# A two-layer hybrid block in fp32 on one core: the Hyena stage cut into nine short steps a block, with the filters' last layer as fp32r in two halves

## The chip, the cores and the metric

The kernel runs on one core of a Trainium2 chip. The metric is the device time of one execution in microseconds. Each engine of the core (TensorE or PE, VectorE or DVE, ScalarE or ACT, GpSimd or POOL, and SyncE or SP, which here only issues DMAs) runs its own program in order; they meet through semaphores.

## The reference

Two layers over 256 tokens of width 2048. Nearly all the work is dense products with weights. Beside them stand, in the first layer, a Hyena branch and an mLSTM branch, in the second layer two further mixers. The change touches the Hyena branch alone:

```
...
    h = jnp.sin(f1.astype(f32) * (z @ w1.astype(f32) + b1.astype(f32)))
    h = jnp.sin(f2.astype(f32) * (h @ w2.astype(f32) + b2.astype(f32)))
    h = h @ w3.astype(f32)
...
    return h.reshape(L, HYENA_ORDER, 2, HYENA_WIDTH) * window[:, None, None, :]
...
def long_conv(u, kf, bias):
    L = u.shape[1]
    uf = jnp.fft.rfft(u, n=2 * L, axis=1)
    y = jnp.fft.irfft(uf * kf[None], n=2 * L, axis=1)[:, :L]
    return y + u * bias
...
        z = hx1 * long_conv(hv, kf[:, 0], hb[0])
        y_a = (hx2 * long_conv(z, kf[:, 1], hb[1])).astype(x.dtype)
```

w3 is 64 x 4096. The filters are two orders by four quarters of 256 channels: eight blocks.

## The kernel before

Every weight matrix streams through SBUF in DMAs of 1 MB (RAW). One such piece is two units, and a unit is eight tiles of 128x128 (`tiles` walks over them, `w.i` counts them). For each unit u, ACT rounds the raw weights to fp32r (WH, L1144), and the rest, raw minus WH, goes to WL: on DVE for even u (L1747), on POOL for odd u (L2557). The activations are split in the same way (HNH and HNL), and `group` multiplies in fp32r WH by HNH (L599), WH by HNL (L600) and WL by HNH (L603). WH and WL have four slots. ACT's program rounds unit v+3 where its own walk comes to tile 8v, but first waits until PE has finished unit v-1. DVE and POOL make the WL of unit v+3 at tile 8v+1, after the WH. So the three stay close to PE's place, and SP issues the next raw piece when both WL of the piece before in that buffer are done.

Beside this stream, a class `Walk` runs a generator ("side") on each engine: `beside(side, rate, skip)` sets how many of its steps fall on 16 tiles and how many are left out first. Every engine has its own `hyena()` with the same count of steps, so step n stands at the same tile in all five programs (on PE after the four tiles it is in). The projections of the first layer (56 pieces, 896 tiles, fourteen groups of 64 tiles) carry the Hyena stage.

Before the change the rate is 1.04 steps on 16 tiles (1.12 from tile 385 on): a step on 15.4 or 14.3 tiles. Three steps make the small network (PE L684 and L690, DVE's range reduction, ACT's sine) and the filters of block 0. A block then has six steps (five for the last):

- step 0: PE transposes the inputs (L707) and transforms the filters (KT, L713); ACT copies both (L1193, L1199); POOL adds and subtracts the halves (KS, L2597 and L2598)
- step 1: PE transforms the inputs (L720), ACT copies one half (L1204), DVE makes UP (L1853)
- step 2: DVE multiplies M (L1859) and adds Y (L1862)
- step 3: DVE multiplies and subtracts the second half (L1866, L1869), POOL adds and subtracts Y into UP (L2604, L2605)
- step 4: PE multiplies the next block's filters, `filters`, 64x128 by 64x512 in fp32 (L677); DVE windows them (L1815); POOL makes HSD (L2583, L2584); SP loads WIN and W3
- step 5: PE's inverse transform (L735), DVE gates the result (L1884, L1890 or L1893), and for the last four blocks ACT and DVE split it into YAH and YAL

In several steps, then, one engine waits for another within the step. In group g, two further things stand at fixed tiles: at tile 16 PE transposes the outputs of the group before (`turn_projected`, L617), and at tiles 18 to 22 ACT and DVE do a short convolution on them (L1433, L1797, L1802).

PSUM: three banks for the stream, five (PB3 to PB7) in turn for everything beside it; PE waits before it takes a side bank until what was in it five turns earlier has been read.

## Time and profile before

| | us |
|---|---|
| median of 3 runs | 2712.99 (2712.69 to 2713.46) |
| the profiled execution | 2712.05, its span 2710.1 |
| PE busy | 2669.4, 98% of the span |
| ACT busy, POOL busy, DVE busy | 1245.3, 1173.8, 1028.0 |
| granted TensorE clock, mean | 0.999 |
| DMA | 488 MB, the queue of the loads busy 50.8% |

PE is busy nearly throughout, in all 40 slices of the page but the first; ACT, POOL and DVE less than half of the time, the DMA engines about half. A busy PE is still not a PE at its peak: two matmuls of the stream that follow each other overlap in the records (0.39 us each, started every 0.227 us), so time is better counted from one start to the next.

### The profile page before, as it was taken

To read this page: it belongs to the slowest core of one execution; us is meant where nothing else is said; L and a number is where in the kernel's file an instruction comes from. 1 tells how busy PE (TensorE), PEld (TensorE's weight loads), DVE (VectorE), ACT (ScalarE), POOL (GpSimd) and SP (SyncE) were. 2 spreads that over 40 slices of the span, in tenths; PEclk is the share of its full clock that TensorE was granted. 3 is DMA by queue.
4 is the path that set the end of the run, shared out by engine and by line. 5 is a ranking of instruction groups with operands and counts; after the bars stand their busy time and mean duration, and the time that the engine had idled before them with its cause. 6 is when DMAs were issued, how large, how long until landed. Compare 5 with 4: busy or idle time off the path is not lost.

```text
span 2710.1 us, 30629 instructions
## 1 busy us (share of the span) xinstructions
PE 2669.4 (98%) x12282; PEld 2197.0 (81%) x12282; DVE 1028.0 (38%) x1262; ACT 1245.3 (46%) x1584; POOL 1173.8 (43%) x535
## 2 busy tenths in 40 slices
PE   8999999999999999999999999999999999999999
PEld 6778777778888888888888878888788888888887
DVE  5556544443432223222233357335432222232222
ACT  5445444444444444444344465555454444444333
POOL 2555553344444444444444446333344444444443
PEclk9999999999999999999999999999999999999999
DMA  6444444355555555555555544454355555555554
GB/s 243 159 150 175 147 153 164 139 206 189 194 185 187 190 187 192 191 192 186 192 192 206 201 156 146 150 202 140 126 186 188 196 190 188 186 188 194 201 199 151
DMA packets 73436, 488.01 MB, mean 180 GB/s; under 512 B 8475, under 2 KB 10428, under 8 KB 15952
## 3 DMA queue, kind: packets, MB, share of 16 engines
q1 hardware_dynamic: 73296, 486.06, 50.8%
q8 instruction: 98, 1.61, 0.2%
q14 instruction: 42, 0.34, 0.0%
HBM read 483.93 MB, written 2.10 MB: 179 GB/s over the span
## 4 chain that ended last, share of the span: by engine, by line
PE 92%; DVE 2%; ACT 2%; issue 2%; POOL 1%; DMA 1%; SPq 0%; ACTq 0%; DVEq 0%; POOLq 0%
PE PB L599 28%; PE PB L603 28%; PE PB L600 28%; PE PB L617 2%; ACT WH L1144 1%; POOL WL L2557 1%; DVE WL L1747 1%; PE PB L713 1%; PE PB L720 1%; PE PB L848 0%; PE PB L735 0%; PE PB L965 0%; DMA RAW<-in_w_in_a 0%; PE PB L808 0%; DVE VY L2422 0%
## 5 line engine op out<-in xcount | busy, mean ns | idle before, releaser
L2557 POOL TENSOR_TENSOR WL<-RAW,WH 128x1024 fp32r<-128x1024 f32 x441 | 1070.2, 2427 | 1451.5 <-ACT WH L1144 1451.5
L1144 ACT ACTIVATE WH<-RAW 128x1024 fp32r<-128x1024 f32 x889 | 940.0, 1059 | 1270.6 <-PE PB L603 1256.4
L1747 DVE TENSOR_TENSOR WL<-RAW,WH 128x1024 fp32r<-128x1024 f32 x448 | 588.8, 1315 | 1522.1 <-ACT WH L1144 1521.8
L599 PE MATMUL PB<-WH,HNH 128*128 128x512 f32 x2464 | 974.2, 395 | 12.4 <-DVE MIX L2359 4.6
L603 PE MATMUL PB<-WL,HNH 128*128 128x512 f32 x2464 | 961.3, 390 | 9.1 <-POOL WL L2557 4.9
L600 PE MATMUL PB<-WH,HNL 128*128 128x512 f32 x2464 | 959.6, 389 | 0.0
L599 PEld LDWEIGHTS PB<-WH,HNH 128*128 128x128 f32 x2464 | 462.8, 188 | 120.3 <-issue 15.4
L603 PEld LDWEIGHTS PB<-WL,HNH 128*128 128x128 f32 x2464 | 462.7, 188 | 109.3 <-POOL WL L2557 6.6
L600 PEld LDWEIGHTS PB<-WH,HNL 128*128 128x128 f32 x2464 | 463.0, 188 | 92.9
L599 PE MATMUL PB<-WH,HDH 128*128 128x512 f32 x704 | 274.3, 390 | 0.0
L603 PE MATMUL PB<-WL,HDH 128*128 128x512 f32 x704 | 273.9, 389 | 0.0
L600 PE MATMUL PB<-WH,HDL 128*128 128x512 f32 x704 | 273.9, 389 | 0.0
L599 PEld LDWEIGHTS PB<-WH,HDH 128*128 128x128 f32 x704 | 132.1, 188 | 27.4
L603 PEld LDWEIGHTS PB<-WL,HDH 128*128 128x128 f32 x704 | 132.1, 188 | 27.4
L600 PEld LDWEIGHTS PB<-WH,HDL 128*128 128x128 f32 x704 | 132.2, 188 | 27.2
L599 PE MATMUL PB<-WH,MXH 128*128 128x512 f32 x128 | 50.1, 392 | 0.0
L603 PE MATMUL PB<-WL,MXH 128*128 128x512 f32 x128 | 49.8, 389 | 0.0
L600 PE MATMUL PB<-WH,MXL 128*128 128x512 f32 x128 | 49.8, 389 | 0.0
L617 PE MATMUL PB<-IDENT,TM 128*128 128x128 f32 x320 | 41.5, 273 | 0.1
L617 PEld LDWEIGHTS PB<-IDENT,TM 128*128 128x128 f32 x320 | 37.1, 140 | 5.5 <-DVE TM L2494 0.4
L2321 DVE TENSOR_TENSOR HDL<-PB,HDH 128x512 fp32r<-128x512 f32 x44 | 28.3, 686 | 13.8 <-ACT HDH L1555 13.8
L2397 DVE SCALAR_TENSOR_TENSOR TM<-PB,RTOK,TM 128x512 f32<-128x512 f32 x44 | 30.9, 743 | 0.0
(357 smaller groups left out, 1790.6 us busy)
## 6 DMA issues: line engine op xcount, KB each, us to landing
RAW<-in_w_gu SPq DMA_DIRECT2D x176, 1024.0 KB, 4.7
RAW<-in_w_dn SPq DMA_DIRECT2D x88, 1024.0 KB, 4.7
RAW<-in_w_in_a SPq DMA_DIRECT2D x55, 1024.0 KB, 4.8
RAW<-in_w_in SPq DMA_DIRECT2D x45, 1024.0 KB, 4.7
RAW<-in_w_out SPq DMA_DIRECT2D x32, 1024.0 KB, 4.7
RAW<-in_w_ga SPq DMA_DIRECT2D x24, 1024.0 KB, 4.7
RAW<-in_w_gb SPq DMA_DIRECT2D x24, 1024.0 KB, 4.7
WIN<-in_win SPq DMA_DIRECT2D x8, 512.0 KB, 5.9
```

The costliest lines, as they stand in the source:

```text
L599: e.matmul(o, hi[:, k, x], WH[:, s, c], start=k == 0, stop=False)
L600: e.matmul(o, lo[:, k, x], WH[:, s, c], start=False, stop=False)
L603: t = e.matmul(o, hi[:, k, x], WL[:, s, c], start=False, stop=k == K - 1)
L617: t = e.transpose(b[:, 256 * i + 128 * h:256 * i + 128 * h + 128], src[:, h, k:k + 128], IDENT[:, :])
L713: e.matmul(bank[:, ri * 256:(ri + 1) * 256], DF[:, c, ri, :], HSD[:, ri, c, :], start=True, stop=True).then_inc(*hy.pe.mark(("kt", blk, c, ...
L720: e.matmul(banks[c][:, ri * 256:(ri + 1) * 256], DF[:, c, ri, :], UT[:, c, :, :].rearrange("p a n -> p (a n)"), start=True, stop=True).the ...
L1144: e.activation(WH[:, u % NSPL, :], RAW[:, n % NRAW, half * SU * 128:(half + 1) * SU * 128], ACT.Copy).then_inc(*wt.act.mark(("wh", u)))
L1747: e.tensor_tensor(WL[:, u % NSPL, :], RAW[:, n % NRAW, half * SU * 128:(half + 1) * SU * 128], f32(WH[:, u % NSPL, :]), ALU.subtract).then ...
L2321: e.tensor_tensor(flat(dst[0][:, k:k + 2, :]), bank(*name, g, q)[:, :], f32(flat(dst[1][:, k:k + 2, :])), ALU.subtract).then_inc(*m.dve.ma ...
L2397: e.scalar_tensor_tensor(out=SIG[:, h, :], in0=mb(nt)[:, 0:512], scalar=RTOK[:, h:h + 1], in1=SIG[:, h, :], op0=ALU.mult, op1=ALU.mult).th ...
L2557: e.tensor_tensor(WL[:, u % NSPL, :], RAW[:, n % NRAW, half * SU * 128:(half + 1) * SU * 128], f32(WH[:, u % NSPL, :]), ALU.subtract).then ...
```

## The change

The diff does four things.

1. The Hyena stage has nine steps a block at a rate of 1.66 on 16 tiles, a step on 9.64 tiles, from tile 74 on. Nearly every result that another engine needs is used a step after it is made. The blocks' order is that of before, and the whole stage takes 86.7 tiles a block.
2. The last layer of the filters is done in fp32r. H2 and HS have 128 rows: the second half of HS holds what the first half lost in rounding. W3 is loaded twice, on 128 rows; ACT rounds it (W3H), DVE takes the rest (W3L). Two fp32r matmuls of 128x128 by 128x512 take the place of one in fp32 of 64x128 by 64x512.
3. The constants are loaded in order of use: the small network's, IDENT, the first filters, then the transforms' matrices.
4. YAH and YAL and the gating move to steps of the next block.

```diff
-        W3 = ar("W3", [64, 2, T], 36)
+        W3 = ar("W3", [128, 2, T], 36)
+        W3H = ar("W3H", [128, 2, T], 50, F32R)
+        W3L = ar("W3L", [128, 2, T], 75, F32R)
+        HS = ar("HS", [128, T], 86, F32R)
...
-            w.beside(hyena(), 1.04, 7)
+            w.beside(hyena(), 1.66, 4)
...
# tensor: filters
-                        e.wait_ge(*hy.act.done("sin", 1))
-                        e.wait_ge(landed["w3"], 16 * (q + 1))
-                    e.matmul(bank[:, :], H2[:, c * 128:(c + 1) * 128], W3[:, :, :].rearrange("p a n -> p (a n)"),
-                             start=True, stop=True).then_inc(*hy.pe.mark(("fw", q, c)))
+                        e.wait_ge(*hy.dve.done("hs"))
+                        e.wait_ge(*hy.dve.done("w3l", q))
+                    e.matmul(bank[:, :], HS[:, c * 128:(c + 1) * 128], flat(W3H[:, :, :]), start=True, stop=False)
+                    e.matmul(bank[:, :], HS[:, c * 128:(c + 1) * 128], flat(W3L[:, :, :]), start=False,
+                             stop=True).then_inc(*hy.pe.mark(("fw", q, c)))
...
# tensor: a block (kt at step 0, bu at 2, filters at 5, inv at 8)
                     yield
+                    yield
                     banks = [wide_bank("bu", blk, 0), wide_bank("bu", blk, 1)]
...
-                    yield
-                    yield
-                    yield
+                    yield from idle(3)
                     if blk < 7:
                         filters(blk + 1)
-                        yield
+                    yield from idle(3)
                     bank = wide_bank("inv", blk)
...
# scalar: step 1 of a block, after the copies of UT and KT
+                    if blk < 7:
+                        filter_high(blk + 1)
+                    if blk >= 5:
+                        gated_high(blk - 1)
+                    yield
...
# vector: a block
+                for blk in range(8):
+                    if blk:
+                        gated(blk - 1)
+                    yield
+                    yield
+                    if blk >= 5:
+                        gated_low(blk - 1)
+                    yield
+                    if blk < 7:
+                        filter_low(blk + 1)
+                    yield
+                    e.wait_ge(*hy.act.done("bu0", blk))
...
# then UP; yield; M and Y of the first half; yield; of the second half; yield; filters(blk + 1); yield; yield
...
# gpsimd: KS at step 2, Y into UP at step 7, spectra(blk + 1) at step 8
-                    yield
-                    yield
-                    yield
+                    yield from idle(5)
                     a, b = flat(Y[:, 0, :, :]), flat(Y[:, 1, :, :])
```

On POOL the sum over Y (UP<-Y) and the spectra of the next filters (HSD) now stand in neighbouring steps. The places are blocks 1 and 2; WL is the stream's. First before, then now:

```order
30 L2557 TENSOR_TENSOR WL<-RAW,WH 128x1024 x3
31 L2604 TENSOR_TENSOR UP<-Y 128x512
32 L2605 TENSOR_TENSOR UP<-Y 128x512
33 L2557 TENSOR_TENSOR WL<-RAW,WH 128x1024
34 L2583 TENSOR_TENSOR HSD<-FW 128x256
35 L2584 TENSOR_TENSOR HSD<-FW 128x256
```

```order
30 L2604 TENSOR_TENSOR WL<-RAW,WH 128x1024 x3
31 L2650 TENSOR_TENSOR UP<-Y 128x512
32 L2651 TENSOR_TENSOR UP<-Y 128x512
33 L2630 TENSOR_TENSOR HSD<-FW 128x256
34 L2631 TENSOR_TENSOR HSD<-FW 128x256
```

In this block the WL that stood between the two is gone from there.

On DVE, in block 0, the convolution (X<-PB,VEC,X) stood between the two halves of M and Y, and now stands ahead of both. Before:

```order
57 L1859 TENSOR_TENSOR M_81<-UP,KSP 128x1024
58 L1862 TENSOR_TENSOR Y<-M_81 128x2x256
59 L1797 SCALAR_TENSOR_TENSOR X_72<-PB,VEC,X_72 128x255 x2
60 L1802 SCALAR_TENSOR_TENSOR X_72<-PB,VEC,X_72 128x255 x2
61 L1797 SCALAR_TENSOR_TENSOR X_72<-PB,VEC,X_72 128x255 x2
62 L1802 SCALAR_TENSOR_TENSOR X_72<-PB,VEC,X_72 128x255 x2
63 L1747 TENSOR_TENSOR WL<-RAW,WH 128x1024
64 L1866 TENSOR_TENSOR M_81<-UP,KSP 128x1024
65 L1869 TENSOR_TENSOR Y<-M_81 128x2x256
```

Now:

```order
59 L1922 TENSOR_TENSOR UP<-KT,PB 128x512 x2
60 L1807 SCALAR_TENSOR_TENSOR X_72<-PB,VEC,X_72 128x255 x2
61 L1812 SCALAR_TENSOR_TENSOR X_72<-PB,VEC,X_72 128x255 x2
62 L1807 SCALAR_TENSOR_TENSOR X_72<-PB,VEC,X_72 128x255 x2
63 L1812 SCALAR_TENSOR_TENSOR X_72<-PB,VEC,X_72 128x255 x2
64 L1757 TENSOR_TENSOR WL<-RAW,WH 128x1024
65 L1928 TENSOR_TENSOR M_84<-UP,KSP 128x1024
66 L1931 TENSOR_TENSOR Y<-M_84 128x2x256
67 L1935 TENSOR_TENSOR M_84<-UP,KSP 128x1024
68 L1938 TENSOR_TENSOR Y<-M_84 128x2x256
```

Both halves of M and Y follow one WL, with nothing between them.

On PE, in block 0, the filters of block 1 stand between matmuls of the stream (L595, L596 and L599 of the new kernel are L599, L600 and L603 of the old). Before, then now:

```order
366 L600 MATMUL PB<-WH,HNL 128x512
367 L603 MATMUL PB<-WL,HNH 128x512
368 L677 MATMUL PB<-W_77,H_84 128x512 x2
369 L599 MATMUL PB<-WH,HNH 128x512
370 L600 MATMUL PB<-WH,HNL 128x512
```

```order
345 L596 MATMUL PB<-WH,HNL 128x512
346 L599 MATMUL PB<-WL,HNH 128x512
347 L673 MATMUL PB<-W3H,HS 128x512
348 L674 MATMUL PB<-W3L,HS 128x512
349 L673 MATMUL PB<-W3H,HS 128x512
350 L674 MATMUL PB<-W3L,HS 128x512
351 L595 MATMUL PB<-WH,HNH 128x512
```

Four fp32r matmuls stand for two in fp32.

## Rows read from the trace of the kernel before

**Rows 1.** The page's part 1: busy us (share of the span) xinstructions.

```profile
PE 2669.4 (98%) x12282; PEld 2197.0 (81%) x12282; DVE 1028.0 (38%) x1262; ACT 1245.3 (46%) x1584; POOL 1173.8 (43%) x535
```

**Rows 2.** One stretch: us, busy (count) PE, PEld, DVE, ACT, POOL; clock, DMA, GB/s.

```profile
40.00:420.00 380.00, 369.76 (x1749) 296.48 (x1748) 204.45 (x255) 176.24 (x235) 202.21 (x118) 1.00 0.45 160
```

**Rows 3.** PE's waits of 40:420 in its timeline: start, us, instruction [idle before].

```profile
67.83 0.50 PE L599 MATMUL PB<-WH,HNH 128*128 128x512 f32 x1 [1.36 <-ACT TM L1420]
86.91 1.97 PE L713 MATMUL PB<-HSD,DF 128*128 128x256 f32 x8 [0.94 <-POOL HSD L2584]
118.58 0.50 PE L603 MATMUL PB<-WL,HNH 128*128 128x512 f32 x1 [1.32 <-POOL WL L2557]
...
323.77 0.50 PE L603 MATMUL PB<-WL,HNH 128*128 128x512 f32 x1 [1.31 <-POOL WL L2557]
332.90 0.50 PE L599 MATMUL PB<-WH,HNH 128*128 128x512 f32 x1 [0.69 <-ACT VT L1473]
...
397.37 2.02 PE L735 MATMUL PB<-DG,UP 128*128 128x128 f32 x16 [3.29 <-POOL UP L2605]
```

**Rows 4.** PE's timeline around the first filters (L677).

```profile
77.53 0.39 PE L603 MATMUL PB<-WL,HNH 128*128 128x512 f32 x1
77.85 1.98 PE L677 MATMUL PB<-W,H 64*128 64x512 f32 x4
79.76 0.50 PE L599 MATMUL PB<-WH,HNH 128*128 128x512 f32 x1
80.10 0.40 PE L600 MATMUL PB<-WH,HNL 128*128 128x512 f32 x1
```

**Rows 5.** The chain that ended last, in order of time: start, us, what.

```profile
128.86 1.73 PE PB L713 x8
131.97 0.87 PE PB L617 x8
...
162.13 1.78 PE PB L735 x16
...
900.10 0.88 PE PB L617 x8
944.52 0.87 PE PB L617 x8
```

**Rows 6.** POOL's timeline around block 0's sum over Y, and the last block's.

```profile
102.78 3.21 POOL L2557 TENSOR_TENSOR WL<-RAW,WH 128x1024 fp32r<-128x1024 f32 x1 [2.34 <-ACT WH L1144]
112.74 2.21 POOL L2604 TENSOR_TENSOR UP<-Y 128x512 f32<-128x512 f32 x1 [6.75 <-DVE Y L1869]
114.91 1.29 POOL L2605 TENSOR_TENSOR UP<-Y 128x512 f32<-128x512 f32 x1
...
394.74 1.26 POOL L2604 TENSOR_TENSOR UP<-Y 128x512 f32<-128x512 f32 x1 [3.02 <-DVE Y L1869]
395.96 1.26 POOL L2605 TENSOR_TENSOR UP<-Y 128x512 f32<-128x512 f32 x1
```

**Rows 7.** PE's timeline: the transposes at tile 208, the last block's L720.

```profile
101.38 1.04 PE L617 MATMUL PB<-IDENT,TM 128*128 128x128 f32 x8
...
378.57 1.67 PE L720 MATMUL PB<-UT,DF 128*128 128x256 f32 x7
```

**Rows 8.** DVE's timeline, Y of block 0 and of block 6.

```profile
103.77 2.78 DVE L1862 TENSOR_TENSOR Y<-M 128x512 f32<-128x512 f32 x1
...
346.30 0.69 DVE L1862 TENSOR_TENSOR Y<-M 128x512 f32<-128x512 f32 x1
```

**Rows 9.** Groups by line of 40:420: count, busy us, mean ns, idle before.

```profile
L1199 ACT ACTIVATE KT<-PB 128x512 f32<-128x512 f32 x16 | 9.6, 597 | 4.3 <-PE PB L713 4.1
...
L1859 DVE TENSOR_TENSOR M<-UP,KSP 128x1024 f32<-128x1024 f32 x8 | 9.8, 1219 | 0.1
L1797 DVE SCALAR_TENSOR_TENSOR X<-PB,VEC,X 128x255 f32<-128x255 f32 x16 | 6.9, 473 | 4.3 <-ACT X L1433 4.3
...
L2583 POOL TENSOR_TENSOR HSD<-FW 128x256 f32<-128x256 f32 x16 | 13.8, 860 | 3.9 <-DVE FW L1815 3.9
```

More of the change, by code:

```diff
@@ L689, in hyena @@
                 e.wait_ge(*hy.act.done("sin", 0))
-                e.matmul(bank[0:64, 0:T], FW1[0:64, 64:128], H2[:, :], start=True,
+                e.matmul(bank[:, 0:T], FW1[0:64, 64:192], H2[0:64, :], start=True,
                          stop=True).then_inc(*hy.pe.mark(("f", 1)))
-                yield
+                yield from idle(4)
                 filters(0)
-                yield
+                yield from idle(3)
                 for blk in range(8):
@@ L738, in hyena @@
                     yield
+                yield from idle(3)
             def heads_turned(h):
@@ L1205, in hyena @@
                                  ACT.Copy).then_inc(*hy.act.mark(("bu0", blk), frees("bu", blk, 0)))
[L1206 to L1216 removed]
+                    yield from idle(6)
+                yield
+                gated_high(7)
+                yield
+                yield
             def mlstm():
@@ L1449, in scalar @@
             for g in range(10):
-                if g == 6:
-                    w.beside(w.side, 1.12)
                 for k in tiles(64):
@@ new lines, in gated_low @@
+                def gated_low(blk):
+                    for j in (2 * blk - 8, 2 * blk - 7):
+                        e.wait_ge(*hy.act.done("ya", j))
+                        e.tensor_tensor(YAL[:, j, :], X2[:, j, :], f32(YAH[:, j, :]), ALU.subtract).then_inc(
+                            *d.mark(("ya", j), *(["end"] if j == 7 else [])))
+                yield
+                reduced(0)
+                yield from idle(3)
+                reduced(1)
+                yield
+                yield
@@ L2282, in vector @@
             low(1)
-            w.beside(hyena(), 1.04, 7)
+            w.beside(hyena(), 1.66, 4)
             for g in range(10):
-                if g == 6:
-                    w.beside(w.side, 1.12)
                 for k in tiles(64):
@@ L2587, in hyena @@
             def hyena():
-                yield
-                yield
+                yield from idle(9)
                 spectra(0)
@@ L2608, in hyena @@
                         spectra(blk + 1)
-                        yield
                     yield
+                yield from idle(3)
             def levels():
@@ L2655, in gpsimd @@
             e.memset(EPSC[:, 1:2], 128.0 * EPS).then_inc(*m.pool.mark("eps"))
-            w.beside(hyena(), 1.04, 7)
-            for k in tiles(24 * 16):
+            w.beside(hyena(), 1.66, 4)
+            for k in tiles(56 * 16):
                 if k % 4 == 1 and 12 <= k < 40:
                     add_square(0, k // 4 - 2)
-            w.beside(w.side, 1.12)
-            e.wait_ge(*m.pe.done("squares", 0, 1))
-            e.memset(VT[:, :, :, 256:257], 1.0).then_inc(*ml.pool.mark("vt ones"))
-            run(32 * 16)
+                if k == 24 * 16:
+                    e.wait_ge(*m.pe.done("squares", 0, 1))
+                    e.memset(VT[:, :, :, 256:257], 1.0).then_inc(*ml.pool.mark("vt ones"))
             w.rest()
```

167 lines of the change are left out of this document (90 added, 77 removed).

## The prediction, made before the changed kernel had run

> **What bounds the kernel now.** First the page's busy times: PE works in 98% of the span, no other engine in half of it [rows 1]. So the kernel is bound by what PE issues, and a change can help in two ways only: fewer or shorter instructions on PE, or less waiting of PE. Then the stretch that holds the Hyena stage, 40 to 420 us: PE is busy for 369.76 of 380.00 us and idle for 10.24, while DVE, ACT and POOL are each busy for about half [rows 2]. Then PE's own timeline of that stretch, which says where the 10.2 us are [rows 3]: 1.36 where ACT was late with a group's result; 0.94 for the first spectra; three times 1.3 for a WL that POOL made late (two are shown, the third stands at 204.00); 0.69 for VT; and 3.29 for the last block's inverse transform, which waits for POOL's sum over Y. They add up to 10.2. The rest of the kernel, 2290 us after it, is not touched.
>
> A clock for the argument comes from two transposes of the same kind in the feed-forward part: 44.42 us from one to the next, of which 0.88 are theirs, with 192 stream matmuls between, so 43.54 / 192 = 0.227 us for one [rows 5]. Four tiles hold six matmuls, so a tile of the stream is 0.340 us.
>
> **The filters on PE.** The last stream matmul before the filters starts at 77.53, the first after them at 79.76, the second at 80.10 [rows 4]. Undisturbed, these would be 0.227 and 0.227 apart, so the two fp32 matmuls cost (79.76 - 77.53 - 0.227) + (0.34 - 0.227) = 2.00 + 0.11 = 2.11 us. The four in fp32r have the shape of the stream's (128x128 by 128x512): 4 x 0.227 = 0.91, and no change of precision on either side. Saved: 1.20 us a block, 8 blocks, 9.6 us. These lie on the bounding engine, so they come off the time. The lower end is 4 matmuls with the 0.11 kept on each side, 8 x (2.00 - 0.91 - 0.11) = 7.8; the upper end is 9.6 plus nothing, since a fp32r matmul of this shape has never been shorter here.
>
> The Trainium skill, "FP8 and Floating Point Precision", section "TensorE Precision Notes", says that true fp32 takes four passes through the array; by that rule four fp32r matmuls stand against eight passes and save 8 x 4 x 0.227 = 7.3 us, an estimate that would make the sum 2703.3; the trace has 2.00 + 0.11 instead of 1.82, the rest being the change-over, and I take the trace.
>
> The other PE instructions of the stage keep count and kind. The second small product gets 128 columns of weights instead of 64, with the same 256 moving columns: nothing.
>
> **What is added beside PE.** ACT: one copy of 128x512 a block for W3H, about 0.6 by the copies of KT [rows 9]. DVE: one subtraction of 128x512, 0.69 by Y where it is undisturbed, up to 2.78 where it isn't [rows 8]. Together about 5 us of ACT and 5.5 (at most 22) of DVE in 380 us in which both idle for about half; PE's stream hides them, as long as WH and WL come in time. SP loads 256 KB instead of 128 for W3, into a queue that is busy for 0.45 of the stretch [rows 2]; nothing. Loads in order of use: nothing in the sum, as no wait for these loads stands among the seven [rows 3]. I allow -0.5 to +1 for all of this.
>
> **The waits of before.** The 1.36 goes: ACT was held in the sine, for which DVE had not been ready; now the sine stands a step behind. The 0.94 goes: the first spectra have a step more and stand far ahead of their use. The three of 1.3 have one cause: POOL waits 6.75 us in its program for Y, and the WL behind it comes late [rows 6]. With two halves of M and Y back to back on DVE, and the sum over Y a step later, POOL enters its wait later and holds no WL. So these 3.95 go too. The VT wait of 0.69 stays.
>
> **What is late next.** The new steps are short: 9.64 tiles are 3.28 us of stream. A result that is used one step later has that, plus what PE has beside the stream in it. POOL's sum over Y takes 1.30 + 1.29 = 2.6 us undisturbed [rows 6]; before, it had two steps until PE's inverse transform in seven blocks of eight, now it has one. And where a WL of POOL's falls just ahead, it goes first. In group 3 PE comes to tile 208 at 101.38 [rows 7], and POOL's WL of the unit that ACT rounds there starts at 102.78, 1.40 later [rows 6]; alone it takes 2.40. So in such a unit POOL's sum ends 1.4 + 2.4 + 2.6 = 6.4 us after PE reached the unit's first tile. From the rates I get the tiles of the steps:
>
> - Block 3: POOL's WL at tile 497, the sum at 498, the inverse transform at 508. PE needs 12 tiles, 4.1 us. Wait 6.4 - 4.1 = 2.3.
> - Block 1: WL at 321, sum at 325, inverse at 336: 16 tiles, 5.4 us. Wait 1.0.
> - Block 6: 753, 758, 768: the same, 1.0.
> - Blocks 2 and 4: no such WL, or 20 tiles and transposes between: none.
> - Blocks 0, 5, 7: DVE is late instead. Block 0: convolution until about 5.9 us after tile 208, WL to 7.1, M and Y twice (2 x 1.22 + 2 x 0.69, [rows 8, 9]; one Y delayed by POOL) to 12.9, sum to 15.5; PE is at tile 248 after 40 x 0.340 + 0.87 for the transposes [rows 5] + 0.91 for the filters = 15.4. Wait 0.1 to 0.3. Block 5 in the same way 0.3, block 7 0.8.
>
> Together 2.3 + 1.0 + 1.0 + 0.3 + 0.3 + 0.8 = 5.7. One bank is late as well: in block 2 the second transform of the filters, at tile 344, takes the bank of the inverse transform of block 1 (tile 336), which DVE frees in its step at tile 344, behind the convolution of group 5 (eight instructions of 0.47 in pairs, [rows 9]): about 8.5 us after tile 336 against PE's 7.4, wait 1.1. The spectra have room except in block 4 (0.2). With VT's 0.7: 5.7 + 1.1 + 0.2 + 0.7 = 7.7 us of waiting, against 10.2: a gain of 2.5.
>
> The bounds of that term: if every new wait is hidden, only VT's 0.7 stays, a gain of 9.5. If DVE and POOL hold each other up at each sum (Y 2.78 instead of 0.69), seven blocks wait 2.1 more than worked out: a loss of 12. I take the worked-out value, since four of eight blocks have Y undisturbed at 0.69 or a slack.
>
> **The sum.** Against the profiled execution's own time: 2712.05 - 9.6 - 2.5 = 2699.95, and it lies 0.94 below the median of the runs, which gives 2700.9. I say 2701.
>
> **Rivals.**
> 1. The waits all go. Nine short steps leave each result one step, and ACT, DVE and POOL run their step at the head of a unit, up to 2.4 us before PE is there. For it: half of each engine is idle. Against it: POOL's WL at tile 497, one tile ahead of the sum. Time 2713.0 - 9.6 - 9.5 = 2693.9.
> 2. The lock. DVE's Y of 512 columns took 0.69 us in block 6 and 2.78 in block 0 while POOL's WL ran, which itself took 3.21 [rows 6, 8]. The change adds eight subtractions of two SBUF inputs on DVE, which can be held up in the same way, about 2.1 us each, and POOL with them; if half of these fall where DVE is the late one, PE waits 4 more: 2701 + 4 = 2705. This is the rule that speaks against the change in the Trainium skill, "SBUF — State Buffer", section "SBUF: two separate sides": DVE with two SBUF inputs and a GpSimd instruction take their shared port in turn, each for a whole instruction. By that rule, the trace agrees.
> 3. Slower than before. The last block of before is the only one that had fewer tiles from the input's transform (tile 816, 378.57 [rows 7]) to the inverse, 40 instead of some 62; there PE waited 3.29 for the sum [rows 3]. Now each block has 57.8, but in six steps with one handover each. If the chain of handovers through ACT, DVE and POOL is late in every block as it was there, 8 x 3.29 = 26.3, plus 0.7 and 1.1: 28.1 of waiting, 17.9 more than before, less 9.6: 2721. It decides from a mean wait of (9.6 + 10.2 - 1.8) / 8 = 2.25 us a block on. Against it: from L720 to the end of the sum it took 22 us in block 0 and 18.6 in the last, and now PE is 57.8 x 0.340 + 1.73 + 0.91 + 0.87 = 23.2 us away.
> 4. The edit to fp32r does not do what it says: its operands wait or the array is slower at 128 rows. Then 0 to 5 of the 9.6 come, about 2707. Against it: the stream itself is of that form.
>
> **Chances.** Forecast (2697.5 to 2703.5) 0.52; rival 1 0.20; rival 2 0.15; rival 3 0.04; rival 4 0.04; the rest spread. The likeliest one's own range is 2697.5 to 2703.5; the one that holds the time 8 times in 10 takes in rival 1 and rival 2: 2693.5 to 2708. A run of this kernel can be told from no change from 0.2% on, 5.4 us, so faster means below 2707.6. Faster 0.90, same 0.06, slower 0.04.
>
> **What would show it.** Right: four fp32r matmuls at PE's filters, the next stream matmul about 1.1 us after the last before them, not 2.2; no wait of PE for WL in the stage; waits at the inverse transform in blocks 3, 1 and 6, in this order of size; one at the second transform of block 2; PE idle for 6 to 10 us from 40 us to the end of the stage; the stage shorter by about 12 us and the rest the same within 1 us. Wrong: idle time there under 3 us (rival 1), or waits over 2 us in most blocks (rival 3), DVE's subtractions at 2.8 us with PE's waits behind them (rival 2), or a change in the time after 420 us.

## The result, and the profile after

| | before | after |
|---|---|---|
| median of 12 runs | 2713.56 (2711.80 to 2716.71) | 2720.08 (2718.55 to 2721.25) |
| the profiled execution | 2712.05 | 2720.57, its span 2718.7 |
| mean granted clock of its TensorE | 0.999 | 0.996 |

The ratio is 1.0021, with a 95% interval from 1.0013 to 1.0028. The change makes the kernel 6.5 us slower; 2701 and "faster" were forecast. The forecast was wrong in its sign, and the time lies outside its range. The two profiled executions are 8.5 us apart, not 6.5, since the one of before is among the fastest of its kernel. In the runs below single executions stand far above the others of their kernel (6966 us in e8, 2731 in e9, 2911 and 9345 in the kernel before beside them); they hardly move a median, but e9's interval is wide by its one.

Part 1 of the page after, which answers to [rows 1] (busy us, share of the span, instructions):

```profile
PE 2668.9 (98%) x12282; PEld 2206.6 (81%) x12282; DVE 1045.0 (38%) x1271; ACT 1246.2 (46%) x1593; POOL 1182.2 (43%) x535
```

Nothing stands out there: PE is busy for 0.5 us less, in a span 8.6 us longer. The stretches of the kernel after tell more (us, busy us and count of PE, PEld, DVE, ACT, POOL; clock, DMA share, GB/s):

```profile
40.00:420.00 380.00, 359.51 (x1711) 298.53 (x1711) 219.20 (x262) 173.19 (x239) 208.36 (x117) 0.98 0.45 158
```

Against [rows 2] PE is idle for 20.5 us instead of 10.2, and its clock is 0.98 instead of 1.00. Both are new, and only the first had a term in the forecast. PE's waits in that stretch, from its timeline (start, us, instruction, idle before and what ended it), which answer to [rows 3]:

```profile
113.72 2.02 PE L731 MATMUL PB<-DG,UP 128*128 128x128 f32 x16 [0.71 <-POOL UP L2651]
154.76 2.95 PE L731 MATMUL PB<-DG,UP 128*128 128x128 f32 x16 [3.26 <-POOL UP L2651]
...
238.36 3.75 PE L731 MATMUL PB<-DG,UP 128*128 128x128 f32 x16 [3.93 <-POOL UP L2651]
280.90 2.02 PE L731 MATMUL PB<-DG,UP 128*128 128x128 f32 x16 [1.01 <-POOL UP L2651]
...
364.69 3.75 PE L731 MATMUL PB<-DG,UP 128*128 128x128 f32 x16 [4.21 <-POOL UP L2651]
405.97 2.02 PE L731 MATMUL PB<-DG,UP 128*128 128x128 f32 x16 [2.46 <-POOL UP L2651]
```

These six are the inverse transforms of blocks 0, 1, 3, 4, 6 and 7. Their waits sum to 15.6 us. The other three waits are 0.94 at 164.35 for a bank that DVE's ST frees (block 2), and 1.80 at 203.07 and 2.17 at 330.00 for POOL's spectra (blocks 3 and 6). All nine make 20.5. (Two more at the stage's end, of 0.4 and 0.5 us, stand in every kernel of this document alike and are left out throughout.) The waits of before at WL, for TM, for VT and at the first spectra are gone.

The second column of these rows has the other half of the loss. Sixteen matmuls of L731 take 2.02 us after the waits of 0.71, 1.01 and 2.46, and 2.95, 3.75 and 3.75 after those of 3.26, 3.93 and 4.21. The windows of 10 us around the three show the granted clock (third column from the right):

```profile
150.00:160.00 10.00, 6.74 (x35) 6.06 (x34) 3.84 (x5) 3.52 (x6) 9.05 (x8) 0.83 0.52 184
230.00:240.00 10.00, 6.07 (x28) 5.02 (x27) 5.17 (x6) 2.69 (x3) 8.41 (x6) 0.88 0.65 247
240.00:250.00 10.00, 10.00 (x43) 8.67 (x43) 1.81 (x4) 1.64 (x2) 3.32 (x3) 0.78 0.16 45
360.00:370.00 10.00, 5.79 (x24) 5.01 (x23) 3.40 (x5) 2.38 (x4) 8.54 (x7) 0.69 0.29 106
370.00:380.00 10.00, 10.00 (x46) 8.40 (x45) 2.95 (x5) 3.69 (x6) 1.49 (x1) 0.97 0.30 105
```

The shortfall, 10 us times (1 - clock), is 1.7 + 1.2 + 2.2 + 3.1 + 0.3 = 8.5 us. In the profile before, no such window from 40 us to the end of the stage was under 1.00. What it does to the stream is seen behind the second of the three waits:

```profile
241.76 0.77 PE L595 MATMUL PB<-WH,HNH 128*128 128x512 f32 x1
242.34 0.63 PE L596 MATMUL PB<-WH,HNL 128*128 128x512 f32 x1
242.76 0.63 PE L599 MATMUL PB<-WL,HNH 128*128 128x512 f32 x1
243.19 0.63 PE L595 MATMUL PB<-WH,HNH 128*128 128x512 f32 x1
```

The matmuls start 0.43 us apart instead of 0.227: the lower of the two clock levels, 1.2 GHz.

The filters came out as forecast. PE's timeline around them, which answers to [rows 4]:

```profile
102.20 0.39 PE L599 MATMUL PB<-WL,HNH 128*128 128x512 f32 x1
102.42 0.39 PE L673 MATMUL PB<-W3H,HS 128*128 128x512 f32 x1
102.65 0.39 PE L674 MATMUL PB<-W3L,HS 128*128 128x512 f32 x1
102.88 0.39 PE L673 MATMUL PB<-W3H,HS 128*128 128x512 f32 x1
103.10 0.39 PE L674 MATMUL PB<-W3L,HS 128*128 128x512 f32 x1
103.33 0.39 PE L595 MATMUL PB<-WH,HNH 128*128 128x512 f32 x1
```

103.33 - 102.20 = 1.13 from the last stream matmul before to the first behind, less its own 0.227: 0.90 us for four, where the two in fp32 took 2.11.

**The account.** I measure the stage from PE's first wait for the norm (SQA), at 32.70 us before and 32.75 after, to its first wait for a MIX, at 456.90 and 465.48. That is 424.20 and 432.73 us: 8.5 longer, and the whole span is 8.6 longer. So all of it lies in the stage: -9.6 for the filters, +10.3 for the waits, +8.5 for the clock make +9.2, against 8.5 measured. The shortfall counts a bit too much, since part of the low clock falls into the waiting itself: 1.6 us of it in this trace, so 0.8 is counted twice, and the sum without it is +8.4.

The same terms account for the miss. The forecast for the profiled execution was 2699.95, it took 2720.57: 20.6 us more. The waits are 20.5 - 7.7 = 12.8 of it and the clock, without what fell into waits, 7.7; the filters are as forecast.

### The profile page after: what moved, and what is told of

The parts are those of the page before. It is cut to its first block, busy times and chain, and to the rows that moved or that the text cites. A ratio compares the mean times of both kernels' runs of the same rounds, so it can differ in the third digit from the quotient of the medians.

```text
span 2718.7 us, 30661 instructions
## 1 busy us (share of the span) xinstructions
PE 2668.9 (98%) x12282; PEld 2206.6 (81%) x12282; DVE 1045.0 (38%) x1271; ACT 1246.2 (46%) x1593; POOL 1182.2 (43%) x535
## 4 chain that ended last, share of the span: by engine, by line
PE 90%; DVE 4%; POOL 2%; ACT 2%; issue 1%; DMA 1%; SPq 0%; ACTq 0%; DVEq 0%; POOLq 0%
PE PB L595 28%; PE PB L599 28%; PE PB L596 28%; PE PB L613 2%; ACT WH L1139 1%; PE PB L731 1%; POOL WL L2604 1%; POOL UP L2651 1%; PE PB L718 1%; PE PB L710 1%; DVE WL L1757 0%; PE PB L845 0%; DVE Y L1938 0%; PE PB L805 0%; DMA RAW<-in_w_in_a 0%
## 5 line engine op out<-in xcount | busy, mean ns | idle before, releaser
L595 PE MATMUL PB<-WH,HNH 128*128 128x512 f32 x2464 | 974.6, 396 | 9.2 <-DVE MIX L2406 4.6
L599 PE MATMUL PB<-WL,HNH 128*128 128x512 f32 x2464 | 962.3, 391 | 5.2 <-DVE WL L1757 4.2
L596 PE MATMUL PB<-WH,HNL 128*128 128x512 f32 x2464 | 961.0, 390 | 0.0
L595 PEld LDWEIGHTS PB<-WH,HNH 128*128 128x128 f32 x2464 | 464.1, 188 | 110.8 <-issue 9.9
L599 PEld LDWEIGHTS PB<-WL,HNH 128*128 128x128 f32 x2464 | 463.6, 188 | 104.5 <-DVE WL L1757 5.1
L596 PEld LDWEIGHTS PB<-WH,HNL 128*128 128x128 f32 x2464 | 463.9, 188 | 93.3
L595 PE MATMUL PB<-WH,HDH 128*128 128x512 f32 x704 | 274.3, 390 | 0.0
L599 PE MATMUL PB<-WL,HDH 128*128 128x512 f32 x704 | 273.9, 389 | 0.0
L596 PE MATMUL PB<-WH,HDL 128*128 128x512 f32 x704 | 273.9, 389 | 0.0
L599 PEld LDWEIGHTS PB<-WL,HDH 128*128 128x128 f32 x704 | 132.2, 188 | 27.6
L596 PEld LDWEIGHTS PB<-WH,HDL 128*128 128x128 f32 x704 | 132.2, 188 | 27.3
L595 PEld LDWEIGHTS PB<-WH,HDH 128*128 128x128 f32 x704 | 132.2, 188 | 27.1
L595 PE MATMUL PB<-WH,MXH 128*128 128x512 f32 x128 | 50.1, 392 | 0.0
L599 PE MATMUL PB<-WL,MXH 128*128 128x512 f32 x128 | 49.8, 389 | 0.0
L596 PE MATMUL PB<-WH,MXL 128*128 128x512 f32 x128 | 49.8, 389 | 0.0
L731 PE MATMUL PB<-DG,UP 128*128 128x128 f32 x128 | 20.5, 326 | 15.6 <-POOL UP L2651 15.6
L731 PEld LDWEIGHTS PB<-DG,UP 128*128 128x128 f32 x128 | 19.0, 235 | 18.4 <-issue 18.3
```

Source lines behind the costliest of these rows:

```text
L595: e.matmul(o, hi[:, k, x], WH[:, s, c], start=k == 0, stop=False)
L596: e.matmul(o, lo[:, k, x], WH[:, s, c], start=False, stop=False)
L599: t = e.matmul(o, hi[:, k, x], WL[:, s, c], start=False, stop=k == K - 1)
L731: t = e.matmul(bank[:, k:k + 128], UP[:, c, ri, ct * 128:(ct + 1) * 128], DG[:, ri, c, :], start=ri == 0, stop=ri == 1)
```

## Why POOL's sum was later than worked out

The forecast put block 3's sum at 1.40 + 2.40 + 2.59 = 6.4 us behind PE's arrival at the unit's first tile. POOL's timeline of the kernel after, in block 3:

```profile
231.59 3.20 POOL L2604 TENSOR_TENSOR WL<-RAW,WH 128x1024 fp32r<-128x1024 f32 x1 [2.73 <-ACT WH L1139]
234.74 1.26 POOL L2650 TENSOR_TENSOR UP<-Y 128x512 f32<-128x512 f32 x1
235.97 2.24 POOL L2651 TENSOR_TENSOR UP<-Y 128x512 f32<-128x512 f32 x1
```

PE came to the tile at 230.19; 1.40 later POOL starts its WL, just as forecast. But the WL takes 3.20, not 2.40, and the second half of the sum 2.24, not 1.29. It ends at 238.21, 8.0 us behind PE's arrival, 1.6 later than worked out, and PE's wait is 3.93 instead of 2.3. DVE's timeline of the same time has the partners:

```profile
230.70 0.69 DVE L1938 TENSOR_TENSOR Y<-M 128x512 f32<-128x512 f32 x1
231.31 1.22 DVE L1757 TENSOR_TENSOR WL<-RAW,WH 128x1024 fp32r<-128x1024 f32 x1
...
235.62 1.48 DVE L1757 TENSOR_TENSOR WL<-RAW,WH 128x1024 fp32r<-128x1024 f32 x1 [1.89 <-ACT WH L1139]
```

POOL's WL begins at 231.59 while DVE's WL runs until 232.53, and POOL's second half begins at 235.97 while the next WL of DVE runs until 237.10. Each is lengthened by about the time that DVE's still had to run: the WL by 0.80, with 0.94 left of DVE's, the half of the sum by 0.95, with 1.13 left. In block 6 it is DVE that is held, and POOL then waits for it (first POOL, then DVE):

```profile
356.28 2.91 POOL L2604 TENSOR_TENSOR WL<-RAW,WH 128x1024 fp32r<-128x1024 f32 x1 [2.29 <-ACT WH L1139]
361.08 1.27 POOL L2650 TENSOR_TENSOR UP<-Y 128x512 f32<-128x512 f32 x1 [1.89 <-DVE Y L1938]
362.31 2.24 POOL L2651 TENSOR_TENSOR UP<-Y 128x512 f32<-128x512 f32 x1
```

```profile
356.85 3.42 DVE L1935 TENSOR_TENSOR M<-UP,KSP 128x1024 f32<-128x1024 f32 x1
360.30 0.69 DVE L1938 TENSOR_TENSOR Y<-M 128x512 f32<-128x512 f32 x1
```

M takes 3.42 us instead of 1.22 beside POOL's WL; POOL stands idle for 1.89 until Y is there. Over the stage the groups by line of the kernel after say how often (count, busy us, mean ns, idle before), beside [rows 9] for M, 1219 ns:

```profile
L1938 DVE TENSOR_TENSOR Y<-M 128x512 f32<-128x512 f32 x8 | 16.0, 1995 | 0.3
L1928 DVE TENSOR_TENSOR M<-UP,KSP 128x1024 f32<-128x1024 f32 x8 | 12.5, 1559 | 0.3
...
L1860 DVE TENSOR_TENSOR W3L<-W,W3H 128x512 fp32r<-128x512 f32 x8 | 7.6, 956 | 0.0
```

```profile
L2651 POOL TENSOR_TENSOR UP<-Y 128x512 f32<-128x512 f32 x8 | 14.1, 1763 | 0.0
```

Y of the second half takes 1995 ns in the mean where an undisturbed one takes 690. This is the rule that the prediction weighed as rival 2, from the Trainium skill, "SBUF — State Buffer", section "SBUF: two separate sides": a DVE instruction with two SBUF inputs and a GpSimd instruction (one that reads SBUF) exclude each other for a whole instruction. The trace agrees, with the overlaps above.

The holding-up itself is not new, only its place. Before, the first half of Y took 2.77 us or more in six of eight blocks, but the second half, after which POOL's sum can start, in one. In the kernel after it is three first halves and five second ones (blocks 0, 1, 2, 4 and 7), one M of 3.10 and one of 3.42, and in six blocks half of the sum takes 2.2 instead of 1.3. But in seven of the eight blocks what was lost had two steps to be made up in before the inverse transform, and now it has one.

## The experiments

Twelve kernels were timed, each beside runs of the kernel before on the same chip. For every one I give the median and the ratio to the kernel before with its 95% interval, and behind the last of them stands one table that splits each stage into filters, waits and clock, as above.

**The parts alone.** First the new steps with the filters left in fp32 on 64 rows; second the old steps with the filters in fp32r (L1148 is the WH there); third only the new order of loads.

```diff
# e1: after, without W3H, W3L, HS
-                    e.matmul(bank[:, :], HS[:, c * 128:(c + 1) * 128], flat(W3H[:, :, :]), start=True, stop=False)
-                    e.matmul(bank[:, :], HS[:, c * 128:(c + 1) * 128], flat(W3L[:, :, :]), start=False,
...
+                    e.matmul(bank[:, :], H2[0:64, c * 128:(c + 1) * 128], flat(W3[0:64, :, :]),
+                             start=True, stop=True).then_inc(*hy.pe.mark(("fw", q, c)))
# e2: before, with these lines the other way round, and its six steps a block
# e12: before
-            e.dma_start(IDENT[:, :], A["ident"]).then_inc(landed["ident"], 16)
-            e.dma_start(DF[:, :, :, :], A["df"]).then_inc(landed["df"], 16)
-            e.dma_start(DG[:, :, :, :], A["dg"]).then_inc(landed["dg"], 16)
             e.dma_start(ZT[:, :], A["zt"]).then_inc(landed["zt"], 16)
...
+            e.dma_start(IDENT[:, :], A["ident"]).then_inc(landed["ident"], 16)
             filter_loads(0)
+            e.dma_start(DF[:, :, :, :], A["df"]).then_inc(landed["df"], 16)
+            e.dma_start(DG[:, :, :, :], A["dg"]).then_inc(landed["dg"], 16)
```

> The nine short steps with the filters as before: two fp32 matmuls of 64x128 by 64x512, no W3H, W3L and HS. Main theory (short steps leave POOL's sum over Y too late for the inverse transform, and the long waits are followed by TensorE at its lower clock; the fp32r filters save about 1.1 us a block on PE and cost nothing else): about 2720 + 9 = 2729, with the waits at the inverse transform the same within 2 us (15.6 us) and the same three stretches at the lower clock. Rival (the added splits on ACT and DVE are what makes DVE and POOL late): the waits at the inverse transform fall to below 8 us, the clock stays up, and the time is 2712 to 2718.

Measured: 2721.56, ratio 1.0027 [1.0015, 1.0038]. The steps alone make it slower, by about 7 us. Neither expectation held: the waits at the inverse transform are 11.4 us, neither 15.6 nor below 8, two stretches are at the lower clock, and the time is 7 below the first and 4 above the second. And the kernel with both parts is only 1.5 us faster than this one, a difference within the two intervals, though PE does 9.6 us less in it: PE waits for 14.8 us here and for 20.5 there, and the clock's shortfall is 3.4 here and 8.5 there. In the two traces the stage is not even shorter with fp32r, 432.7 us against 432.3: what the filters save, PE gives back, some 5.7 as waiting and 5 as clock.

> The six long steps of before with the new filters: W3H on ACT in step 1, W3L on DVE in step 2, two fp32r matmuls in the place of each fp32 one. Main theory: 2713.5 - 9.6 = 2704 (2702 to 2707), waits of PE from 40 to 420 us about 10 as before. Rival (the splits load DVE and POOL so that they are late): waits of 14 or more in the stretch and 2709 to 2714.

Measured: 2717.52, ratio 1.0008 [0.9999, 1.0016]. I expected 2704. In the old steps the saving goes the same way: the three waits at WL are 3.12, 3.11 and 3.11 instead of 1.32, 1.32 and 1.31, and the clock is low after four waits. Part of it is the added work, as the rival had it (waits of 14 or more; they are 15.9, though the time lies above its 2714 too): DVE's W3L stands ahead of the second half of Y, and POOL waits for that half 7.35 us in blocks 0, 2 and 5 instead of 6.75 [rows 6]. POOL's row in block 0:

```profile
115.13 2.22 POOL L2637 TENSOR_TENSOR UP<-Y 128x512 f32<-128x512 f32 x1 [7.35 <-DVE Y L1902]
```

So of the 1.8 by which each wait at WL is longer, 0.6 come with W3L, and 1.2 are left, as much as the filters save in a block. The fp32r filters alone, then, gain nothing that can be measured, though PE's instructions are 9.6 us shorter. I had not asked in the forecast whether PE, being at those places the one that waits, can use time that it saves.

> The kernel before with the constants loaded in the changed order and nothing else. All theories: the same as before within 0.5 us of its wait pattern (10.2 us of waits from 40 to 420 us), 2713 to 2714.

Measured: 2714.40, ratio 1.0001 [0.9992, 1.001]: nothing, as expected.

**Is it the waiting at the inverse transform, and what of it is clock?** One kernel puts the inverse transform of a block a step into the next, with the gating behind it; the other has the steps of the kernel after, but fills PE's waits in blocks 1, 3 and 6 with 12, 14 and 14 fp32 matmuls of 128x128 whose result is overwritten.

```diff
# e3: tensor, a block
                     yield                  # behind kt
+                    if blk:
+                        inverse(blk - 1)
                     yield
# e4: tensor, a block, ahead of the wait for POOL's sum
+                    for _ in range({1: 12, 3: 14, 6: 14}.get(blk, 0)):
+                        e.matmul(bank[:, 0:128], ONES[:, :], ONES[:, :], start=True, stop=True)
                     e.wait_ge(*hy.pool.done("z", blk))
```

> The changed kernel with the inverse transform two steps after POOL's sum over Y instead of one (step 1 of the next block; the gating at its step 2, YAH at 3, YAL at 8). Main theory: the waits at the inverse transform go from 15.6 to under 2 us, TensorE stays at its upper clock, and the time is 2720 - 15.6 - 8 + 1 = 2697 (2695 to 2702). If the lower clock has nothing to do with these waits: about 2720 - 15.6 = 2705. Rival (POOL and DVE are overloaded as a whole and the lateness only moves on): the waits turn up at the next consumer (spectra, WL), and the time stays over 2712.

Measured: 2721.57, ratio 1.0028 [1.0017, 1.0039]. The waits at the inverse are gone, and seven stand at the spectra in their place, 18.9 us together. Four of them from PE's timeline:

```profile
201.95 3.75 PE L721 MATMUL PB<-HSD,DF 128*128 128x256 f32 x8 [3.40 <-POOL HSD L2637]
244.81 3.38 PE L721 MATMUL PB<-HSD,DF 128*128 128x256 f32 x8 [2.36 <-POOL HSD L2637]
287.80 3.75 PE L721 MATMUL PB<-HSD,DF 128*128 128x256 f32 x8 [4.03 <-POOL HSD L2637]
336.09 3.75 PE L721 MATMUL PB<-HSD,DF 128*128 128x256 f32 x8 [4.20 <-POOL HSD L2637]
```

The main expectation of this run failed, and its rival held: a wait taken away at one place uncovers the next result, since the spectra are made on POOL one step before PE wants them. The clock goes with them: the eight matmuls of L721 take up to 3.75 us where undisturbed ones take 1.97 [rows 3].

> The changed kernel with 12, 14 and 14 fp32 matmuls of 128x128 by 128x128 (ONES by ONES, into the bank that the inverse transform then overwrites) ahead of PE's wait in blocks 1, 3 and 6, so that PE is busy for some 3 us of each of the three long waits. They lie inside the waits. Main theory: PE comes on at the same place, but at the upper clock: 2720 - 7.7 = 2712 (2711 to 2715). If the lower clock is not caused by the idle time: 2720, with the low stretches still there.

Measured: 2717.34, ratio 1.0011 [1.0002, 1.002]. PE's timeline in block 3, with the 14 matmuls (28 records) and the inverse transform:

```profile
233.40 3.29 PE L727 MATMUL PB<-ONES 128*128 128x128 f32 x28
...
237.39 2.05 PE L733 MATMUL PB<-DG,UP 128*128 128x128 f32 x16 [0.70 <-POOL UP L2653]
```

PE is kept from its own work for just as long (3.29 + 0.70 = 3.99 us, before that 3.93), yet the sixteen matmuls take 2.05 instead of 3.75, and from 230 to 250 us the clock is 1.00. The stage is 5.6 us shorter than that of the kernel after, the shortfall 6.8 less. This shows by itself that the low clock is a consequence of the idling and has a price of its own. The median gains only 2.7 of it, less than the 5 to 9 that were expected. The eleven runs spread from 2713.57, at a mean clock of 0.999, to 2720.92, at 0.996, and the profiled one has lost clock behind the stage too; that the low clock comes at other places in some executions would explain the difference, but there is a trace of one execution only.

**POOL's sum.** If POOL is late because its WL and the sum over Y queue up and are held by DVE, the sum belongs to DVE, right behind Y. Four kernels do this: from the kernel after, from the old steps with fp32r filters, from the new steps with fp32 filters, and from the kernel before. A fifth instead gives DVE the WL of the three units (43, 65, 97) that fall ahead of the sums of blocks 1, 3 and 6.

```diff
# e5 to e8, vector, behind Y of the second half (and gone from gpsimd)
+                    a, b = flat(Y[:, 0, :, :]), flat(Y[:, 1, :, :])
+                    e.wait_ge(*d.prev())
+                    e.tensor_tensor(flat(UP[:, 0, :, :]), a, b, ALU.add).then_inc(*d.mark())
+                    e.tensor_tensor(flat(UP[:, 1, :, :]), a, b, ALU.subtract).then_inc(*d.mark(("zz", blk)))
# e11
-            return (wt.pool if u % 2 and u > 7 else wt.dve).done("wl", u)
+            return (wt.pool if u % 2 and u > 7 and u not in (43, 65, 97) else wt.dve).done("wl", u)
```

> The changed kernel with the sum and the difference over Y (into UP) made by DVE right behind Y, in its step 6, instead of by POOL in step 7. POOL is left with WL, KS and HSD. Theory P (POOL is the late link: WL, sum and spectra stand in one queue behind each other, 8 to 10 us from the unit's start): the waits at the inverse transform and at the spectra, 20.5 us in the changed kernel, fall below 5, no stretch at the lower clock is left, and the time is 2695 to 2701. Rival D (DVE is the late link, or the two engines hold each other up in any case): DVE has 11 to 20 us more to do, WL and Y come later, waits stay over 10 us, and the time is 2708 or more.

Measured: 2708.76, ratio 0.9981 [0.9972, 0.999], 11 us faster than the kernel after by this one edit. Waits 12.8 us, shortfall 3.4. That is what rival D expected (over 10 us, 2708 or more), not theory P: POOL's sum was late, but taking it away is not enough. The waits at the inverse transform fall from 15.6 to 6.0 (1.99 and 2.36 of them in the last two blocks); those for the spectra and their bank grow from 4.9 to 6.8, the longest 3.21 in block 6.

> The six long steps of before with the fp32r filters (as in the run of the filters alone) and the sum over Y on DVE. Theory P: the three WL waits of 3.1 us and the last inverse transform's 3.3 go, since POOL no longer waits for Y; waits of 4 or less, about 2697 (2695 to 2702). Rival D: waits of 8 or more and over 2706.

Measured: 2709.41, ratio 0.9978 [0.997, 0.9987]. With the sum on DVE, old and new steps do not differ: the intervals overlap nearly fully. Rival D again has the numbers: the waits are 11.7 us.

> The nine short steps with the old fp32 filters, the sum over Y on DVE. Theory G (the PE time that the fp32r filters save is real, and was given back as a longer wait for POOL): with POOL's lateness gone, this kernel is slower than the one with fp32r filters and the same steps by the whole 9 us (8 to 10): about 2706. Rival (fp32r filters save PE nothing that counts): the two are the same within 3 us, as the changed kernel and its version with fp32 filters were (2720.1 and 2721.6).

Measured: 2712.80, ratio 0.9994 [0.9985, 1.0003]. Against e5 the fp32r filters now bring 4.0 of the 9.6 us, more than the rival's 3 and far less than the 8 to 10 of theory G. In the two traces the waits are 8.2 with fp32 and 12.8 with fp32r, the shortfall 0 and 3.4, and the stage is only 1.7 us shorter with fp32r.

> The kernel before with the sum over Y on DVE and nothing else. Theory P: the WL waits (3.95 us) and the last wait (3.29) go, 2713.5 - 7 = 2706 (2704 to 2709). Rival D: 2712 or more.

Measured: 2713.79, ratio 0.9993 [0.9984, 1.0002]: on the kernel before, the same edit gains nothing that can be measured, as rival D had it. The waits at WL are gone as expected, but the last block's inverse waits 4.24 us instead of 3.29 (DVE's M ahead of it takes 3.39 instead of 1.21), and the clock is 0.66 from 390 to 400 us.

> The changed kernel with the low halves of units 43, 65 and 97 (those that stand on POOL just ahead of the sum over Y of blocks 1, 3 and 6) made by DVE. Theory W (this WL ahead of the sum makes it late): the waits at the inverse transform in blocks 1, 3 and 6 (3.26, 3.93, 4.21) fall to under 1.5 each, no lower clock behind them; 2720 - 9 - 7 = 2704 (2702 to 2709). Rival (DVE's second Y is the later of the two): these waits stay above 2.5, and the time above 2714.

Measured: 2712.83, ratio 0.9993 [0.9985, 1.0002], 7 us faster than the kernel after. The three waits in PE's timeline are now:

```profile
152.32 2.02 PE L731 MATMUL PB<-DG,UP 128*128 128x128 f32 x16 [1.15 <-POOL UP L2651]
...
232.27 2.02 PE L731 MATMUL PB<-DG,UP 128*128 128x128 f32 x16 [1.62 <-DVE FW L1825]
...
354.58 3.75 PE L731 MATMUL PB<-DG,UP 128*128 128x128 f32 x16 [3.04 <-POOL UP L2651]
```

3.26, 3.93 and 4.21 became 1.15, 1.62 and 3.04, and the clock is kept at the first two. The three don't all fall below 1.5, and the time is above the 2702 to 2709 of theory W, below the 2714 of its rival. The WL ahead of the sum was the larger part of blocks 1 and 3, but not of block 6. The sum is still held: POOL's two halves in block 3 read

```profile
227.71 2.20 POOL L2650 TENSOR_TENSOR UP<-Y 128x512 f32<-128x512 f32 x1 [2.61 <-DVE Y L1938]
229.87 2.26 POOL L2651 TENSOR_TENSOR UP<-Y 128x512 f32<-128x512 f32 x1
```

since DVE now has two WL in a row beside them. (The sum ends at 232.13; what PE's row names, DVE's FW, which frees the bank, ends at 232.19, so there the bank is as late as the sum.)

**A version that moves everything that was late.** From e5: the inverse transform in the next block's step 1, and the filters a step earlier all through (PE 4, DVE 6, POOL 7), so that the spectra have a step between them and their use. Beside it the same with fp32 filters.

```diff
# e9: tensor, a block
                     yield                  # behind kt
+                    if blk:
+                        inverse(blk - 1)
                     yield
...
-                    yield from idle(3)
+                    yield from idle(2)
                     if blk < 7:
                         filters(blk + 1)
# vector: filters(blk + 1) ahead of the second half of M, filter_low(blk + 1) ahead of gated(blk - 1)
# gpsimd: spectra(blk + 1) one step earlier
```

> The changed kernel with the sum over Y on DVE, the inverse transform at step 1 of the next block (gating 2, YAH 3, YAL 8), and the next block's filters a step earlier (PE 4, DVE 6, spectra on POOL 7). So every product of DVE and POOL that PE waited for has two steps. If lateness against a one-step distance is the cause: waits from 40 to 420 us under 4 (12.8 with the sum on DVE alone), no stretch at the lower clock, 2696 to 2702. If DVE and POOL are short of time as a whole: waits of 8 or more, at other places, and 2706 or more.

Measured: 2704.13, ratio 0.9968 [0.9952, 0.9985], the fastest of all: 10.7 us below the kernel before on the same chip, and some 14 below the kernel after by the two ratios. It lies between the two expectations, and so do its waits, 6.0 us. PE's waits in the stage are three:

```profile
230.53 0.50 PE L599 MATMUL PB<-WL,HNH 128*128 128x512 f32 x1 [2.69 <-DVE WL L1763]
315.21 0.50 PE L599 MATMUL PB<-WL,HNH 128*128 128x512 f32 x1 [3.02 <-DVE WL L1763]
388.08 0.50 PE L599 MATMUL PB<-WL,HNH 128*128 128x512 f32 x1 [0.25 <-DVE WL L1763]
```

None is for the Hyena stage's own results any more; now DVE, which has taken over the sum, is late with the stream's WL.

> The same arrangement with the old fp32 filters. Theory G (the 9 us that fp32r filters save on PE count in full only where PE does not wait for DVE and POOL anyway): 7 to 10 us slower than the version with fp32r filters. Rival (half of the saving is always lost): 4 or less, as between the two versions with the sum on DVE (2708.8 and 2712.8).

Measured: 2707.95, ratio 0.9977 [0.9968, 0.9987], 3.8 slower than e9 where theory G expected 7 to 10; its rival's "4 or less" has the number. In the stage the difference is 6.8 us: 9.6 less the 2.7 by which e9 waits longer. The other 3 come behind the stage, where e9's trace has lost clock at waits that both kernels have:

```profile
520.00:540.00 20.00, 17.07 (x61) 12.80 (x60) 9.44 (x14) 6.48 (x6) 6.90 (x3) 0.84 0.46 157
540.00:560.00 20.00, 20.00 (x87) 16.53 (x86) 8.94 (x17) 7.57 (x9) 7.07 (x3) 0.93 0.29 106
```

In the trace of e10 these two windows are at 1.00 and 0.91.

**All of them in one account.** "Stage" is the stage's length against that of the kernel before, 424.20 us, from SQA to MIX. "Waits" is PE's waiting in it less 10.2; "clock" is the shortfall, ten us times (1 - clock) over the windows of 10 us from 40 us to its end. The sum of the three should be the stage.

| kernel | median us | stage | filters | waits | clock | sum |
|---|---|---|---|---|---|---|
| after | 2720.08 | +8.5 | -9.6 | +10.3 | +8.5 | +9.2 |
| e1 steps only | 2721.56 | +8.1 | 0 | +4.6 | +3.4 | +8.0 |
| e2 fp32r only | 2717.52 | +1.6 | -9.6 | +5.7 | +6.8 | +2.9 |
| e3 inverse later | 2721.57 | +9.5 | -9.6 | +8.7 | +13.6 | +12.7 |
| e4 busy wait | 2717.34 | +2.9 | -9.6 | +10.8 | +1.7 | +2.9 |
| e5 sum on DVE | 2708.76 | -3.9 | -9.6 | +2.5 | +3.4 | -3.7 |
| e6 old steps, fp32r, sum on DVE | 2709.41 | -5.8 | -9.6 | +1.5 | +3.4 | -4.7 |
| e7 new steps, fp32, sum on DVE | 2712.80 | -2.2 | 0 | -2.1 | 0 | -2.1 |
| e8 before, sum on DVE | 2713.79 | -0.8 | 0 | -2.0 | +3.4 | +1.4 |
| e9 all moved | 2704.13 | -13.0 | -9.6 | -4.3 | +1.7 | -12.2 |
| e10 all moved, fp32 | 2707.95 | -6.2 | 0 | -6.9 | +1.7 | -5.2 |
| e11 three WL on DVE | 2712.83 | -1.2 | -9.6 | +5.0 | +3.4 | -1.2 |
| e12 load order | 2714.40 | +1.4 | 0 | 0 | +1.7 | +1.7 |

(In e4 the 40 added matmuls count as waiting, 3.29 / 14 = 0.235 us each, 9.4 in all.) The sum meets the stage within 1 us in nine of thirteen, and lies too high in the other four, by 1.1 to 3.2. Part of that is low clock that fell into waiting: PE waited for 4.9 us of it in e3, 2.2 in e8, 1.8 in e6 and 0.7 in e2, and half of these stretches (the lower clock is half of the upper) is counted twice. With it taken off the sum, all thirteen meet the stage within 1.1 us. So three terms are enough to tell where the time of each of these kernels went. In the whole time one more thing moves: whether the clock is lost behind the stage too, which the traces of e4 and e9 show.


## Why the prediction was wrong, point by point

1. **What bounds the kernel.** Right: PE, and only PE's instructions and waits. But PE's speed was left out as a third way. The profile before had one sign of it, the 3.29 us wait at 397 us [rows 3]: its sixteen matmuls took 2.02 us, so that idling seemed to cost nothing but itself.
2. **The filters, 9.6 us.** The term is right on PE: 0.90 us a block instead of 2.11, and between e9 and e10 the stage differs by 6.8 + 2.7 = 9.5 us. As a gain in time it was wrong: a saving on PE counts only as far as PE doesn't wait for another engine next. With POOL late it brought 1.5 us (after and e1, within the noise), with the sum on DVE 4.0 and 4.4 (e5 against e7, e6 against e8), with everything moved 3.8.
3. **The waits of before.** Right: those for TM, the first spectra and WL went. VT's 0.69, which was to stay, went too.
4. **What is late next.** This is the step of the forecast that failed first: 7.7 us of waiting, 20.5 measured, and it is mostly one of size. Most places were right (blocks 3, 1 and 6 at the inverse, block 2 at the bank, there 0.94 against 1.1), and POOL's start in block 3 as well. The sizes were taken from undisturbed durations: 2.3, 1.0 and 1.0 for blocks 3, 1 and 6 became 3.93, 3.26 and 4.21. The prediction had the disturbed ones, a Y of 2.78 and a WL of 3.21 [rows 6, 8], and named "a loss of 12" for the end at which DVE and POOL hold each other up at each sum; it chose the other value, "since four of eight blocks have Y undisturbed". Measured was a loss of 10.3. That count does not come out of the trace of before, where six blocks have the first half of Y held and one the second, and the choice had no ground in the order of the instructions: the change puts DVE's M, Y and WL and POOL's WL and sum into the same few us, and each of the eight blocks has at least one instruction that is held. e11 (POOL's WL taken away: two of the three waits down by 2.1 and 2.3) and e5 (the sum taken from POOL: 11 us faster) show that POOL's queue of WL and sum is what the inverse transform waits for. That the part above the forecast is the holding-up rests on the overlaps in the trace; no kernel was timed that has the same work on both engines and no overlap. The rest of the miss is smaller waits: block 7's 2.46 instead of 0.8, block 4's 1.01 where none was worked out, and the spectra (1.80 and 2.17 us), which weren't named in these blocks at all and queue behind the sum and the WL.
5. **The clock.** This is the second step that failed: the sum has no term for it. The trace has 8.5 us of shortfall, and e4 shows by itself that it goes when PE is kept busy for the same time.
6. **The rivals.** Rival 1 (no waits) did not come; e9, with three, is the nearest to it. Rival 2 named the right mechanism and the wrong carrier: W3L took 956 ns in the mean, 0.27 above an undisturbed Y, 2 us in all; M, Y, WL and the sum made the rest. Rival 3 had 0.04 and came out nearest, 2721 against 2720.08, with 28.1 us of waiting; measured were 20.5 of waiting and 8.5 of lost clock, so its time is right by a different sum. Rival 4 did not occur.

Block 1's 2.3 us above the forecast are three parts: 0.95 in the second half of the sum, 0.6 in POOL's wait for Y, and 0.7 because POOL's WL starts later. PE comes to the unit at 145.90 and POOL's WL starts at 148.04, 2.14 behind it and not 1.40: ACT rounds this WH only at 146.90, behind two copies of TM.

What stays open: in e2, e8 and e10 the stage is still some 1 us shorter than the sum, with the double count taken off.

## What to carry to other kernels

Before a saving on the bounding engine is counted, look at what that engine waits for next: while it waits for a partner, a shorter instruction only makes the wait longer, and the partner's chain is to be shortened first; here one edit to that chain (the sum on DVE) was worth 11 us in the kernel after and made 4 of the filters' 9.6 us count. It gained nothing on the kernel before (e8), so the chain to shorten is to be read anew after each change. Where two engines that can hold each other up get work in the same few microseconds, take the disturbed duration that the trace already shows, not the mean or the undisturbed one. And price a wait of PE above its own length, by the slow instructions behind it.
